# Queries made in turned form for pairs of token tiles in the projection stage of an MLA and pooling step

## The reference, cut to what matters

```
h = rmsnorm(x, g_pre)
z = h @ w_in                     # q_lat 256, kv_lat 128, k_r 64, then the gate and pool parts
q = (rmsnorm(q_lat, g_q) @ w_uq).reshape(b, L, 8, 128 + 64)
q_r   = rope(q[..., 128:], pos)  # 8 heads x 64: x1*cos - x2*sin, x2*cos + x1*sin
q_abs = einsum('bshn,rhn->bshr', q[..., :128], w_uk)    # 8 heads x 128
ckv_new = rmsnorm(kv_lat, g_kv)
kr_new  = rope(k_r, pos)
```

## Time and profile before

| | us |
|---|---|
| median of 3 runs | 2246.03 (2244.46 to 2247.4) |
| the profiled execution | 2245.05 |
| its span | 2243.3 |
| TensorE matmul busy in the span | 2154.3 (96%) |
| VectorE, ScalarE, GpSimd busy | 1294.8, 1010.7, 355.6 |
| mean granted TensorE clock | 0.984 |

### The profile page before, as it was taken

How to read it: one execution, slowest core, us unless ns; L and a number is a source line. 1 busy time by engine, 2 the same in 40 slices (tenths; PEclk the granted TensorE clock), 3 DMA queues, 4 the chain that set the end, 5 groups by cost and what they waited for, 6 DMA issues and landing times.

```text
span 2243.3 us, 32505 instructions
## 1 busy us (share of the span) xinstructions
PE 2154.3 (96%) x11994; PEld 1989.9 (89%) x11994; DVE 1294.8 (58%) x2646; ACT 1010.7 (45%) x1797; POOL 355.6 (16%) x496
## 2 busy tenths in 40 slices
PE   6999789999999999799999999999999999999997
PEld 6888668888888888579999999999999999999997
DVE  5565468788877778345534464446444564446434
ACT  5555545555555555344333443344333433344233
POOL 2333311110011010105000410014000510032000
PEclk9999799999999999899999999999999999999999
DMA  5454422111110021443444345344534344333532
GB/s 197 156 167 149 130 66 57 43 35 37 29 29 24 19 74 45 147 136 122 153 147 136 120 135 174 112 143 134 177 119 143 119 141 160 128 113 126 174 122 69
DMA packets 131001, 252.80 MB, mean 113 GB/s; under 512 B 17898, under 2 KB 80882, under 8 KB 129702
## 3 DMA queue, kind: packets, MB, share of 16 engines
q1 hardware_dynamic: 109214, 221.05, 30.2%
q10 hardware_dynamic: 19344, 17.30, 2.8%
q0 software_dynamic: 2304, 12.58, 1.5%
HBM read 208.34 MB, written 42.79 MB: 112 GB/s over the span
## 4 chain that ended last, share of the span: by engine, by line
PE 53%; POOL 1%; DVE 1%; issue 0%; ACT 0%; POOLq 0%; DVEq 0%; ACTq 0%
PE d_ps L120 53%; PE d_ps L1825 1%; POOL d_win L1668 1%; DVE d_y L1727 0%; DVE d_y L1745 0%; POOL d_fstat L1649 0%; POOL d_fstat L1646 0%; POOL d_t L1680 0%; ACT d_zs L1626 0%; POOL d_t L1679 0%; DVE d_y L1729 0%; POOL d_win L1673 0%; DVE d_y L1810 0%; DVE d_wuv L82 0%; POOLq L1363 0%
## 5 line engine op out<-in xcount | busy, mean ns | idle before, releaser
L120 PE MATMUL d_ps<-d_ht,d_wr 128*128 128x412 f32 x3840 | 738.5, 351 | 1.7 <-PEq L1063 1.7
L120 PEld LDWEIGHTS d_ps<-d_ht,d_wr 128*128 128x128 f32 x3840 | 720.1, 189 | 5.3 <-issue 1.8
L82 DVE TENSOR_TENSOR d_wr<-d_ws,d_wr 128x1024 fp32r<-128x1024 f32 x260 | 320.7, 1234 | 562.7 <-ACT d_wr L1002 562.7
L1002 ACT ACTIVATE d_wr<-d_ws 128x1024 fp32r<-128x1024 f32 x260 | 275.3, 1059 | 611.7 <-PE d_ps L120 601.6
L911 PE MATMUL b_ps<-kt,k_qs 128*128 128x512 f32 (+3 forms) x1600 | 346.4, 374 | 10.3 <-POOL k_qs L82 6.1
L911 PEld LDWEIGHTS b_ps<-kt,k_qs 128*128 128x128 f32 x1600 | 282.2, 195 | 62.6 <-POOL k_qs L82 9.7
L930 PE MATMUL b_ps<-b_pt,kv 128*128 128x512 f32 x816 | 231.2, 414 | 7.4 <-DVE b_pt L82 7.4
L812 ACT ACTIVATE b_p<-b_p,b_bias 128x1024 f32<-128x1024 f32 (+7 forms) x192 | 171.7, 896 | 105.3 <-DVE b_low L873 102.5
L82 DVE TENSOR_TENSOR b_pt<-b_ps,b_pt 128x512 fp32r<-128x512 f32 x272 | 181.9, 688 | 61.9 <-ACT b_pt L819 60.6
L819 ACT ACTIVATE b_pt<-b_ps 128x512 fp32r<-128x512 f32 x272 | 157.0, 597 | 121.6 <-PE b_ps L930 65.8
L120 PE MATMUL d_ps<-d_mrg,d_wr 128*128 128x412 f32 x960 | 189.8, 353 | 0.0
(11 more groups left out here) (194 smaller groups left out, 2141.7 us busy)
## 6 DMA issues: line engine op xcount, KB each, us to landing
d_ws<-in_w SPq DMA_DIRECT2D x260, 512.0 KB, 3.5
out_q<-a_qout SPq DMA_DIRECT2D x17, 768.0 KB, 3.3
a_x<-in_x ACTq DMA_DIRECT2D x17, 512.0 KB, 3.7
out_ht<-a_hf SPq DMA_DIRECT2D x17, 512.0 KB, 4.2
d_hf<-out_ht SPq DMA_DIRECT2D x20, 412.0 KB, 3.6
d_olf<-out_olat SPq DMA_DIRECT2D x40, 206.0 KB, 3.0
k_qf<-out_q SPq DMA_DIRECT2D x32, 256.0 KB, 2.7
k_qf<-out_q SPq DMA_DIRECT2D x128, 64.0 KB, 2.6
```

The lines of the kernel that those rows point to most:

```text
L82: return e.tensor_tensor(low, source, high.bitcast(f32), ALU.subtract)
L120: mm = pe.matmul(out, stationary(a, k), moving(b, k), start=first and k == 0 and a + b == 0, stop=last and k == depth - 1 and a == 1)
L1002: act.activation(ahead["wr"][k % 2][:, 0, :, :], ahead["ws"][k % 4][:, :, :], ACT.Copy).then_inc(ahead["w_hi"], 1)
```

## The change

The queries are made the other way round: blocks of 128 weight columns are the stationary operand and the turned tokens `qt` move. The result has query channels on the rows and tokens in the columns, as it is stored, so that the 12 transposes and their copies go. Two tiles go together (256 columns); the first group has three, of 8, 128 and 128 tokens (264 columns), since the sample tile is now the first tile and brings only its 8 real tokens. A group's queries are made in two halves of 4 heads, one half in each step: 36 matmuls, first the rotary blocks, then the heads, into a ring of four PSUM banks. The rotation is done on rows with a table `turn` that is loaded for each group. Stores go by half and tile.

The core of the diff:

```
+TILES = (NT - 1,) + tuple(range(PT))
+WIDTHS = (NDEC,) + PT * (P,)
+GROUPS_Q = ((0, 1, 2),) + tuple((n, n + 1) for n in range(3, NT, 2))
+RING = 4
+        for half in range(2):
+            for heads in [None] + [tuple(range(a, a + per_bank)) for a in range(0, HG, per_bank)]:
+        part.freed_by = [last[bank] for bank in part.banks if bank in last]
...
+        def halves(i):
+            return [(k, a) for k, members in enumerate(GROUPS_Q) for a in range(2) if members[-1] + 3 + a == i]
...
 PE
+            turn_tokens(0)
+            for i in range(1, LAST_STEP + 1):
+                if i < NT:
+                    turn_tokens(i)
+                if i <= NT:
+                    n = i - 1
+                    pe.wait_ge(ht_ok, n + 1)
...
+                for k, a in halves(i):
+                    pe.wait_ge(nt_lo, GROUPS_Q[k][-1] + 1)
+                    for part in in_half[k, a]:
+                        for other in part.freed_by:
+                            pe.wait_ge(qcos_ok if other.heads is None else qout_a, other.count)
+                        for columns, bank, at in part.blocks:
+                            mm = three_products(pe, ps_q[bank][:, at:at + NQ[k]],
+                                                lambda b, c: wq[:, b, c, columns:columns + P],
+                                                lambda b, c: qt[:, k % 2, b, c, 0:NQ[k]], KQ)
...
-                for group, columns in ((0, QROPE), (1, QROPE + 512), (2, 0)):
-                        three_products(pe, ps_q[group][:, :], lambda a, k: qt[:, a, k, :],
-                                       lambda b, k: wq[:, b, k, columns:columns + 512], KQ).then_inc(q_ok, 1)
 DVE
+            def norm_tokens(n):
+                dve.wait_ge(x_rinv_ok, n + 1)
+                wait(dve, xt_ok, 2 * n)
+                dve.scalar_tensor_tensor(out=h[:, :], in0=x[:, n % 2, :], scalar=x_rinv, in1=gpre[:, :],
+            def tokens(n):
+                dve.wait_ge(hf_ok, 2 * n + 2)
+                wait(dve, lat_ok, n)
+                dve.tensor_copy(ht[:, 0, :, :], hf[:, :, :]).then_inc(ht_hi, 1)
...
+            norm_tokens(0)
+            tokens(0)
+            norm_tokens(1)
+            for part in range(2):
+                dve.wait_ge(wq_hi, part + 1)
...
+                if i + 1 < NT:
+                    norm_tokens(i + 1)
 ACT
+                for k, a in halves(i):
+                    wait(act, q_out[a], stores(k))
+                    for part in copied[k, a]:
+                        act.wait_ge(q_ok, part.number + 1)
...
+                if i + 1 < NT:
+                    square(i + 1)
 SP
+                if 1 <= i < NT:
+                    sp.wait_ge(hf_ok, 2 * i)
+                    sp.dma_start(io["ht"][:, :, at:at + P], hf[:, :, :]).then_inc(h_out, 16)
...
+                for k, a in halves(i):
+                    sp.wait_ge(qout_d, rotated[k, a].count)
+                    sp.wait_ge(qout_a, copied[k, a][-1].count)
+                    for n in GROUPS_Q[k]:
+                        sp.dma_start(io["q"][TILES[n], :, a, :, 0:WIDTHS[n]],
+                                     qout[:, a, :, OFFSET[n]:OFFSET[n] + WIDTHS[n]]).then_inc(q_out[a], 16)
-                    sp.dma_start(io["q"][bass.ds(o, 1), :, :, :].rearrange("a p h t -> p (a h) t"),
-                                 qout[:, :, :]).then_inc(q_out, 16)
```

More of the change, by code:

```diff
@@ L191, in project @@
[L191 to L211, removed]
+        x_in, x_sq, var_ok, x_rinv_ok, xt_ok, hf_ok = (
+            sem("x_in"), sem("x_sq"), sem("var_ok"), sem("x_rinv_ok"), sem("xt_ok"), sem("hf_ok"))
@@ new lines, in project, with stores @@
+        kv_hi = sem("kv_hi")
+        parts = query_parts()
+        in_half = {(k, a): [part for part in parts if (part.k, part.half) == (k, a)]
+                   for k in range(len(GROUPS_Q)) for a in range(2)}
+        rotated = {key: [part for part in some if part.heads is None][0] for key, some in in_half.items()}
+        copied = {key: [part for part in some if part.heads is not None] for key, some in in_half.items()}
+        def stores(k):
+            return 16 * sum(len(members) for members in GROUPS_Q[:k])
@@ L268, in step @@
[L268 to L277, removed]
+            x_norm(0)
@@ L299, in step @@
                                        ALU.add).then_inc(kro_ok, 1)
-                    wait_all(pool, const_in, CONSTS,
-                             (kro_ok, n + 1))
+                    pool.wait_ge(kro_ok, n + 1)
                     pool.tensor_copy(norm[:, K0 + ROPE:K0 + 2 * ROPE], norm[:, K0:K0 + ROPE]).then_inc(kr_ok, 1)
[L304 to L309, removed]
+                if i + 1 < NT:
+                    x_norm(i + 1)
@@ L313, in _, with turned @@
+            def turned(n):
+                wait(act, h_out, 16 * n)
+                wait(act, ht_ok, n)
+                for a in range(2):
+                    act.wait_ge(xt_ok, 2 * n + 1 + a)
+                    act.activation(hf[:, 4 * a:4 * a + 4, :], ps_x[a][:, :], ACT.Copy).then_inc(hf_ok, 1)
             act.wait_ge(half_ok, 1)
             act.activation(warm[:, :], half[:, 0:1], ACT.Square)
[L316 to L332, removed]
@@ L365, in step @@
+            square(0)
+            turned(0)
+            for part in range(2):
+                act.wait_ge(wlat_in[part], 16)
+                act.activation(wlat[:, 0, 4 * part:4 * part + 4, :], wlat_f[:, 4 * part:4 * part + 4, :],
+                               ACT.Copy).then_inc(wq_hi, 1)
+            square(1)
+            for i in range(1, LAST_STEP + 1):
+                if i < NT:
+                    turned(i)
+                if i <= NT:
                     n = i - 1
-                    wait(act, lat_ok, n + 1)
+                    act.wait_ge(lat_ok, n + 1)
@@ L380, in step @@
-                if new:
-                    wait(act, rinv_ok, n + 1)
+                if i == 1:
+                    act.wait_ge(wq_in, 48)
+                    act.activation(wq[:, 0, :, 0:QROPE], wq_f[:, :, :], ACT.Copy).then_inc(wq_hi, 1)
+                    for k in range(KQ):
+                        for a in range(2):
+                            act.wait_ge(absorbed, 2 * k + a + 1)
+                            act.activation(wq[:, 0, k, QROPE + 512 * a:QROPE + 512 * a + 512], ps_q[2 * a + k][:, :],
+                                           ACT.Copy).then_inc(wq_hi, 1)
@@ L390, in _ @@
-            steps(act, step, columns, prepare, ahead=ahead)
+                if i == LAST_STEP:
+                    for u in range(2):
+                        query_high(act, keep, u)
+                for k, a in halves(i):
+                    wait(act, q_out[a], stores(k))
+                    for part in copied[k, a]:
+                        act.wait_ge(q_ok, part.number + 1)
+                        bank, heads, width = part.banks[0], part.heads, NQ[k]
+                        act.activation(qout[:, a, heads[0]:heads[-1] + 1, 0:width],
+                                       ps_q[bank][:, 0:len(heads) * width].rearrange("p (h t) -> p h t", h=len(heads)),
+                                       ACT.Copy).then_inc(qout_a, 1)
@@ L468, in _ @@
-            steps(dve, step, columns, prepare)
+                    dve.wait_ge(ckv_ok, n + 1)
+                    dve.tensor_copy(kv[:, TILES[n], 0, :], norm[:, C0:K0]).then_inc(kv_hi, 1)
+                    dve.wait_ge(kv_hi, n + 1)
+                    split(dve, kv[:, TILES[n], 1, :], norm[:, C0:K0], kv[:, TILES[n], 0, :])
+                if i == 1:
+                    dve.wait_ge(wq_hi, 3)
+                    split(dve, wq[:, 1, :, 0:QROPE], wq_f[:, :, :], wq[:, 0, :, 0:QROPE])
+                    for k in range(KQ):
+                        for a in range(2):
+                            dve.wait_ge(wq_hi, 4 + 2 * k + a)
+                            at = slice(QROPE + 512 * a, QROPE + 512 * a + 512)
+                            low = split(dve, wq[:, 1, k, at], ps_q[2 * a + k][:, :], wq[:, 0, k, at])
+                    low.then_inc(weights_ok, 1)
@@ L542, in _ @@
-            steps(pe, step, prepare=prepare)
+                if i == 1:
+                    pe.wait_ge(wq_in, 48)
+                    for k in range(KQ):
+                        for a in range(2):
+                            for hh in range(4):
+                                head = 4 * a + hh
+                                mm = pe.matmul(ps_q[2 * a + k][:, hh * R:hh * R + R], wuq_t[:, head, k * P:k * P + P],
+                                               wuk_t[:, head, :], start=True, stop=True)
+                            mm.then_inc(absorbed, 1)
```

437 lines of the change are left out of this document (219 added, 218 removed).

## The result

The changed kernel takes 2327.14 us (median of four runs; 2245.9 us for the kernel before in the same runs): 1.036 times the time before, 95% interval 1.0345 to 1.0375. One of the four took 3037.58 us, at a mean granted clock of 0.662 instead of 0.96; without it the median is 2325.54 us, the ratio and its interval are those of the other three, and the profile is of one of them. The prediction was 2322 us, range 2288 to 2340.

The account below looks back on a forecast made before the run. TensorE was taken to bound the projection stage, at 12.18 us per step. The forecast: 2245.05 + 50.6 for the new order at full clock + 25.6 for lost clock = 2321.3, 1.0 higher as median: 2322 us, range 2288 to 2340.

Parts of the forecast that it names:

- step 16: Last of the projection steps, counted as a full step: +2.9 us, and 1.6 us for the clock.
- start to the first latents copy: Start of the projection stage: h of tile 1 stands ahead of VectorE's split of `wlat`, +3.1 us.
- step 1: Projection step with h of tile 2 behind the splits of `wq`: 15.2 us, +1.5, and 1.6 for the clock.
- steps 2 to 4: Projection steps without queries: 12.85 us each against 12.18, together +2.0, and 1.6 each for the clock.
- steps 5, 6: Steps of the 264-column group, whose third head waits for a bank: 18.2 us, +6.0 each, and 1.6 for the clock.
- steps 7 to 15: Full projection steps with queries: 15.1 us at full clock, +2.9 each, and 1.6 each for the clock.
- end: From the last latents copy to attention: four halves of queries, a copy and the last store, 23.9 us, +3.0.
- The loop: Chain per full projection step: queries, last copy, square, power, h, turning, latents product; 15.1 us, TensorE idle 4.2.
- The clock: Lower TensorE clock after each step's idle time: 1.6 us in each of 16 steps, +25.6 us, bounds 0 and 38.
- The stores: Rival: `hf` lands 1 to 2 us late in 12 steps, 12 to 20 us more, about 2337 us; chance 0.12.
- TensorE as the bound: Rival: h comes in time in the projection stage, so the saving stands, about 2227 us; chance 0.04.
- 256 columns: Price of the 36 query matmuls per step: 0.13 us each, 4.7 us, by the trace; 3.9 by the skill page.

Follow-up runs that it names:

- e1: Changed kernel with ScalarE's square of the next tile's x and GpSimd's power moved ahead of the latents' wait and powers; 2314.12 us, ratio 1.0339.
- e2: e1 with VectorE also making the next tile's h before it waits for the latents product; 2318.67 us, ratio 1.0365.
- e3: e2 with the store of hf issued in the tile's own step, ahead of the query and latents stores; 2222.19 us, ratio 0.9929.
- e4: Changed kernel with 16 extra matmuls of 512 columns, results unused, behind each step's queries from step 5 on; 2299.63 us, ratio 1.0278.
- e6: Changed kernel with VectorE's rotation of the queries ahead of the latents' normalising and the low parts; 2318.03 us, ratio 1.0324.
- e7: e3 with e6's rotation first, the start ordered as before the change, and the last copies of heads ahead of attention's high parts; 2225.07 us, ratio 0.9908.
- e5: Changed kernel with only the store of hf issued in the tile's own step; 2326.44 us, ratio 1.0362.
- e9: e2 with ScalarE's square of the next tile's x ahead of the copies of hf; 2288.22 us, ratio 1.0189.
- e8: e3 with e6's rotation first, without e7's start and end; 2218.69 us, ratio 0.988.

## Why the prediction was right

Right in the sign, the size and the chain, but the size with some luck: one term, step 16, was 7.2 us too large and hid most of the 10.9 us by which the six other terms of the stage were too small. By its own steps, against the trace of the changed kernel (before from its timeline; 1.6 us of clock are in each predicted step):

| term | predicted | measured |
|---|---|---|
| start to the first latents copy | +3.1 | 28.03 - 22.98 = +5.0 |
| step 1 | +3.1 | 17.05 - 13.69 = +3.4 |
| steps 2 to 4 | +6.8 | 44.6 - 36.55 = +8.1 |
| steps 5, 6 | +15.2 | 41.3 - 24.5 = +16.8 |
| steps 7 to 15 | +40.5 | 152.6 - 110.2 = +42.4 |
| step 16 | +4.5 | 9.5 - 12.2 = -2.7 |
| end | +3.0 | 27.7 - 20.9 = +6.9 |
| rest of the kernel | 0 | -0.6 |
| sum | +76.2 | +79.3 |

- **The loop.** Predicted from the end of the product: square at 5.7, h done at 9.15, turning at 9.25. Measured: 5.2, 8.8, 8.9. e1, e2 and e3 show that it is this chain, and that no single link of it was the cause: after the square comes VectorE's queue, after that the store of hf.
- **The clock** was mis-sized: 2.4 us per full step (0.83 in the transposes, 1.57 in the product) instead of 1.6. I took the price from a product behind the idle time and left out the transposes of h that stand between. It is 2.4 in steps 9 to 15; in steps 7 and 8, whose transposes were wholly or partly at full clock, it is 1.7 (granted 0.77 over 7.5 us). Part of it hid behind the loop's being 0.35 us shorter. That filling the idle time takes the low clock away, and that this clock costs 2.4 us of a step, e4 shows.
- **Steps 5 and 6**: e6 shows the wait for the bank; it was priced at 3.1 us and is worth 4.2.
- **The start** was 1.9 us too small. The first latents product began at 21.04 us, 0.4 late, but took 6.58 us where about 5.4 were counted; why is not shown. Behind it the copies of hf waited for the first store until 27.06, and the latents copy stood behind them.
- **Step 16** was wrong in sign: after the last h is turned nothing waits for another one, so the step has its product straight behind the queries. I counted it with the full ones: 7.2 us too much.
- **The end** was 3.9 us too small. The last copies of heads stand behind attention's high parts, which wait for their load (ended 316.5, 4 us after TensorE's last query matmul), a term that I left out; e7 shows that it is not worth what it seems, since GpSimd's low parts end at 319.3 in any case.
- **The stores** as a rival fell: hidden in the changed kernel (e5), but only 1.5 us behind. In e2, e9 and e4 they became the bound. One of the prediction's signs of being wrong was there all the same: the copies of hf do wait for the store's landing, 99.3 us in all. The sign was badly chosen, for that wait ended before the product did and was worth nothing.
- **The other signs**: the granted clock of the stage was 0.83 (0 to 322 us), under the 0.85 to 0.9 expected, steps 5 and 6 took 20.7 us instead of 18 to 20, and attention began at 320.86 instead of 317; h was released by GpSimd's power and TensorE idled 4.2 us, as said.
- **TensorE as the bound** was the right rival to keep for what the change can do: its 2227 us are a ratio of 0.992, and e3 and e8 came to 0.9929 and 0.988. The loss was in the order of the instructions, not in the new form of the queries.
- **256 columns.** 36 matmuls take 4.3 us from start to start, 0.120 us each. The row of before had 0.130. By the formula of the Trainium skill (TensorE: Matmul & The Clock Gate, Back-to-back issue gap) an estimate is 0.109. The measured value lies between, and it decides.

## What to carry to other kernels

In a software pipeline with one buffer per stage, write down for each handover how late it comes after the product that starts the step, and look which of them stand in one chain: moving a producer from beside a long product to ahead of it can cost up to the product's length, however little work was added (here 4.2 us of idle time in each step, beside a product of 5.05). Waits that the profile sums up (99 us for a store) say nothing until the wait that ends last is gone, and then they may be the bound; take them away one by one and together. Idle times of TensorE of 4.2 us were paid twice here, since the work behind them ran at the lower clock.

## What the runs showed of the hardware

- Useless matmuls in an idle time made the kernel 0.8% faster and brought the granted clock from 0.82 to 0.99 (e4). With them idle times of 0.5 to 1.1 us were followed by products of 5.06 to 5.19 us, one of 2.29 us by 6.72, one of 2.58 us by 5.06.
- When h came 0.5 us earlier in e1, the step shortened by 0.2 us only: the clock took the rest back (6.93 us for the product instead of 6.62). Small gains in a chain that contains a low stretch of the clock can't be read at their face value.
- The times of the kernel before differed by 0.3% between two sets of runs (2238.16 and 2244.95), so that only ratios within one set are compared here.
